# First attention of a two-block transformer kernel: far-key scores issued one round earlier, GpSimd's scaling written as a product

## The reference

```python
def block_fn(args):
    q_b, iq_b, iw_b, t_b = args
    ...
    score = jnp.where(causal[None], score, -jnp.inf)
    _, idx = lax.top_k(score, k_top)
    valid = idx <= t_b[None, :, None]
    k_sel = gather(k, idx)
    v_sel = gather(v, idx)
    logits = jnp.einsum("bthd,btkd->bhtk", q_b, k_sel).astype(jnp.float32) * (HEAD_DIM ** -0.5)
    bias = rel_bias[rel_bucket(t_b[None, :, None] - idx)]
    logits = logits + jnp.moveaxis(bias, -1, 1).astype(jnp.float32)
    logits = jnp.where(valid[:, None], logits, -jnp.inf)
    p = jax.nn.softmax(logits, axis=-1).astype(v.dtype)
    o = jnp.einsum("bhtk,btkd->bthd", p, v_sel)
```

## Time and profile before

| | |
|---|---|
| Median of 3 runs | 2642.52 us (2640.56 to 2645.78) |
| Profiled execution | 2639.89 us, span 2638.1 us |
| PE busy | 2502.7 us, 95% |
| DVE, ACT, POOL busy | 1677.6, 955.5, 655.4 us |
| Chain that ended last | PE 80%, DVE 10%, ACT 4% |

### The profile page before, as it was taken

How to read it: one execution, slowest core, us unless ns; L and a number is a source line. 1 busy time by engine, 2 the same in 40 slices (tenths; PEclk the granted TensorE clock), 3 DMA queues, 4 the chain that set the end, 5 groups by cost and what they waited for, 6 DMA issues and landing times.

```text
span 2638.1 us, 32127 instructions
## 1 busy us (share of the span) xinstructions
PE 2502.7 (95%) x12224; PEld 2062.3 (78%) x12224; DVE 1677.6 (64%) x2841; ACT 955.5 (36%) x1767; POOL 655.4 (25%) x536
## 2 busy tenths in 40 slices
PE   5999999988999899999999998999999998999998
PEld 4778888777787678888888886888877776888987
DVE  5499999477424887877654449486596566104843
ACT  4431211377323323223312243332244245225842
POOL 2147522367443000000000130000000044334753
PEclk7999999999999999999999999999999998999999
DMA  4102333200454265664533142323346123533242
GB/s 169 49 22 68 95 97 96 56 2 9 152 183 132 79 211 172 190 191 143 186 119 126 44 133 64 112 72 104 112 175 233 47 64 120 175 111 110 101 155 101
DMA packets 263172, 302.11 MB, mean 115 GB/s; under 512 B 11144, under 2 KB 216428, under 8 KB 263020
## 3 DMA queue, kind: packets, MB, share of 16 engines
q1 hardware_dynamic: 263020, 300.05, 35.0%
HBM read 228.15 MB, written 70.29 MB: 113 GB/s over the span
## 4 chain that ended last, share of the span: by engine, by line
PE 80%; DVE 10%; ACT 4%; DMA 2%; issue 2%; POOL 1%; SPq 0%; POOLq 0%; DVEq 0%; ACTq 0%
PE ps L67 78%; PE ps L70 2%; DVE tmp L79 2%; ACT tmp L73 1%; DVE sm L79 1%; DVE tmp L76 1%; ACT pth L73 1%; DVE wl L76 1%; DVE pwa L76 1%; DVE B2l L76 1%; DVE X L79 0%; DVE ptl L79 0%; ACT bh L73 0%; DVE bl L79 0%; ACT wh L73 0%
## 5 line engine op out<-in xcount | busy, mean ns | idle before, releaser
L76 POOL TENSOR_TENSOR wl<-raw,wh 128x512 fp32r<-128x512 f32 (+1 forms) x224 | 291.0, 1320 | 1590.6 <-ACT wh L73 1590.4
L73 ACT ACTIVATE wh<-raw 128x512 fp32r<-128x512 f32 (+1 forms) x388 | 226.4, 621 | 241.9 <-PE ps L67 177.1
L67 PE MATMUL ps<-B2h,wh 128*128 128x512 f32 x616 | 244.4, 397 | 13.6 <-DVE B2l L76 7.1
L67 PE MATMUL ps<-B2l,wh 128*128 128x512 f32 x616 | 241.4, 392 | 0.0
L67 PE MATMUL ps<-B2h,wl 128*128 128x512 f32 x616 | 241.3, 392 | 0.0
L73 ACT ACTIVATE tmp<-ps 128x512 f32<-128x512 f32 (+5 forms) x164 | 119.2, 738 | 332.3 <-PE ps L67 317.7
L76 DVE TENSOR_TENSOR tmp<-tmp,ps 128x512 f32<-128x512 f32 x204 | 138.4, 685 | 108.4 <-PE ps L67 92.7
L67 PE MATMUL ps<-ah,wh 128*128 128x512 f32 (+1 forms) x608 | 192.1, 393 | 14.0 <-DVE xt L85 9.9
L73 ACT ACTIVATE wh<-ws 128x512 fp32r<-128x512 f32 x152 | 94.4, 627 | 289.2 <-DVE ws L76 262.1
L67 PE MATMUL ps<-B3h,wh 128*128 128x512 f32 x448 | 178.5, 398 | 15.2 <-DVE B3l L76 7.2
L67 PE MATMUL ps<-al,wh 128*128 128x512 f32 (+1 forms) x608 | 190.7, 391 | 0.0
(11 more groups left out here) (290 smaller groups left out, 5785.8 us busy)
## 6 DMA issues: line engine op xcount, KB each, us to landing
ada<-in_ada_w SPq DMA_DIRECT2D x48, 512.0 KB, 3.8
raw<-in_w_in SPq DMA_DIRECT2D x37, 512.0 KB, 4.5
raw<-in_a_w_in SPq DMA_DIRECT2D x33, 512.0 KB, 4.4
gates<-tmp SPq DMA_DIRECT2D x32, 512.0 KB, 3.0
raw<-in_w_ffn_gate SPq DMA_DIRECT2D x24, 512.0 KB, 5.6
hd<-tmp SPq DMA_DIRECT2D x22, 512.0 KB, 4.6
gf<-hd SPq DMA_DIRECT2D x22, 512.0 KB, 7.2
raw<-in_a_w_out SPq DMA_DIRECT2D x20, 512.0 KB, 3.4
```

What stands on the lines that cost most here:

```text
L67: return self.e.matmul(*a, **k) if self.e else Ins()
L73: return self.e.activation(*a, **k) if self.e else Ins()
L76: return self.e.tensor_tensor(*a, **k) if self.e else Ins()
```

## The change

The function `score` of PE now makes one part at a call. Its near part (or the only part, for b below 2) is made at the head of round n as before. Its far part is made by a second entry of the pipeline with lag -1, which stands behind `turn` and ahead of both `values`: so in round n-1. Waits and PSUM ring are the same. On POOL, `norm` is a `tensor_tensor` product with the share spread along the row by `to_broadcast` in place of a `tensor_scalar`.

```diff
-        def score(n):
+        def score(n, part=None):
 
             b, hd = self.ITEMS1[n]
-            if n % 2:
+            parts = self.parts1(b)
+            if n % 2 or part is None and len(parts) == 1:
                 return
...
-            for part, (s0, s1) in enumerate(self.parts1(b)):
-                ps = [self.take(e, ("s", n + k, part), ring=self.p_score) for k in (0, 1)]
...
+            at = 0 if part is None else len(parts) - 1
+            s0, s1 = parts[at]
+            ps = [self.take(e, ("s", n + k, at), ring=self.p_score) for k in (0, 1)]
...
-        pipeline(64, [(0, score), (4, turn), (6, lambda n: values(n, 1)), (5, lambda n: values(n, 0))])
+        pipeline(64, [(0, lambda n: score(n, "near")), (4, turn), (-1, score), (6, lambda n: values(n, 1)), (5, lambda n: values(n, 0))])
...
-                e.tensor_scalar(L[:, 0:W], L[:, 0:W], self.st1(n)[3], None, ALU.mult).then_inc(
+                e.tensor_tensor(L[:, 0:W], L[:, 0:W], self.st1(n)[3].to_broadcast([128, W]), ALU.mult).then_inc(
```

More of the change, by code:

```diff
@@ L1563, in score @@
             c, qh, ql = slice(b * 128, b * 128 + 128), self.qh[hd // 2], self.ql[hd // 2]
-            for part, (s0, s1) in enumerate(self.parts1(b)):
-                ps = [self.take(e, ("s", n + k, part), ring=self.p_score) for k in (0, 1)]
[L1566 to L1569, removed]
+            at = 0 if part is None else len(parts) - 1
+            s0, s1 = parts[at]
+            ps = [self.take(e, ("s", n + k, at), ring=self.p_score) for k in (0, 1)]
+            for i, (q, k) in enumerate(((qh, self.KH), (qh, self.KL), (ql, self.KH))):
+                for p, r in zip(ps, (slice(0, 64), slice(64, 128))):
+                    ins = e.matmul(p[:, 0:s1 - s0], q[r, c], k[r, s0:s1], start=i == 0, stop=i == 2)
+            ins.then_inc(self.sig["prod"].up(*(("prod", ("s", n + k, at)) for k in (0, 1))), 1)
         def turn(n):
```

## The result

The changed kernel takes 2684.5 us (median of 4 executions, 2677.8 to 2688.9); the kernel before took 2641.5 in the same comparison. The ratio is 1.0161, 95% interval 1.0147 to 1.0175: 43 us slower. The forecast had the sign, but 21.9 us of it, and a range that ended at 2669.

The account below looks back on a forecast made before the run. PE, busy 95% of the span, was taken to bound the kernel. Terms 5.1 - 0.4 + 17.2 = 21.9 us on 2639.89 gave 2661.8, with the median's 2.6 us 2664.4; forecast 2663, range 2650 to 2669.

Parts of the forecast that it names:

- The far scores come to wait for `top_far`: On PE in round n-1, far(n) waits for DVE's `top_far` of item n-1: some 20 waits, 0.4 to 1 us each.
- Pairs n = 0 mod 4: First attention, far part ahead of values products on the path: eleven pairs cost 0.21 to 0.62 us, sum 5.1 us.
- Pairs n = 2 mod 4: Far part leaves ACT's shadow and delays values products ACT awaits: 1.12 to 1.70 us per pair, together 17.2 us.
- Sum 21.9 us: Whole first attention: 5.1 - 0.4 + 17.2 us of added time from moving the far parts.
- the list: The prediction's prices per pair for far parts moved a round sooner, such as 0.62 for pair 56, 1.42 for 58.
- The idle before the second part: PE's idle before item 47's second part of the turn: grows from 1.4 to about 2.1 us.
- POOL's product is covered: POOL's scaling falls to 1.9 us at 1024 columns but saves nothing, since a 2.3 us margin before PE's turn covers it.
- rival 4: PE's clock falls as its idles become 2 us: one fall of 10 us costs some 5 us, 2668; chance 0.04.
- Rivals 1 to 3: Waits vanish, lengths count: about +5 (0.06); turn releases ACT: 2642 to 2647 (0.04); faster through POOL: 2628 (0.02).

Follow-up runs that it names:

- e6: The changed kernel with unread matmuls in PE's idles ahead of early far scores and before every fourth transpose's second part: 2667.5 us, ratio 1.0098.
- e1: The kernel before with only POOL's scaling changed to the tensor_tensor product, order of the scores as before: 2641.8 us, ratio 0.9997.
- e5: The changed kernel with unread matmuls only in PE's waits just ahead of each early far score: 2675.8 us.
- e7: The kernel before with 17 unread matmuls in PE's 4.2 us idle at the start of the attention: 2641.3 us, ratio 0.9998.
- e12: The kernel before with far scores sooner only for pairs n = 2 mod 4, plus unread matmuls ahead of them and in the turns' idles: 2664.0 us, ratio 1.0078.
- e3: The kernel before with far scores sooner only for pairs n = 0 mod 4, POOL as before: 2653.3 us, ratio 1.0041.

## Why the prediction was right or wrong

- *The far scores come to wait for `top_far`, behind which stand the values products.* Right: 23 waits, 16.9 us; the longest is 1.9 us, where 1 was forecast.
- *Pairs n = 0 mod 4: 0.61 us each at full width.* Right to the hundredth in the idle (0.61 and 0.61), a little small in its effect: from the turn's second part to ACT's next copy it is 6.67 us (661.66 to 668.33) instead of 5.83, 0.84 more and not 0.62.
- *Pairs n = 2 mod 4: 1.42 for pair 58.* 1.54: from 668.33 to 673.14 are 4.81 us, from 631.21 to 634.48 were 3.27.
- *Sum 21.9 us.* With the clock held up (`e6`) it is 25.8; pair by pair the list was 14% short (21.1 against 18.5), in part because a far part holds PE for 0.9 us and not 0.80. With this error alone the time would have been that of `e6`, 2667.5, inside the range.
- *The idle before the second part grows from 1.4 to about 2.1 us.* Wrong: 1.58 and 1.68 us at 661.66 and 677.44. It did not change the sum.
- *POOL's product is covered.* Right (`e1`). Its price, 1.9 us, was right too. The rule of the Trainium skill (GPSIMD Engine Reference, "Performance versus the Vector engine") that two inputs cost more than one did not hold for this pair of forms: 1892 against 2842 ns.
- *The clock, which the sum holds at 1.00, and rival 4, "One fall of 10 us costs some 5 us: 2668. Chance 0.04".* This is the step that failed. The sum has no term for the clock, and the rival's was too small: the clock did not fall once but in nine stretches after 540 us, and stood 53.5 us longer at half speed than before, which cost 17 us. I had taken the 1.00 of the kernel before as a reason against a fall, though the new order adds idles to the old ones. At narrow widths, where PE before had waited 0.8 to 1.1 us for `ptl`, it now waits longer for the far scores' banks:

```profile
561.46 0.50 PE L67 MATMUL ps<-kp,qh 64*128 64x256 f32 x4 [1.55 <-DVE st L88]
...
572.61 1.00 PE L67 MATMUL ps<-kp,qh 64*128 64x384 f32 x4 [1.69 <-DVE st L88]
...
586.34 1.01 PE L67 MATMUL ps<-kp,qh 64*128 64x384 f32 x4 [1.93 <-DVE st L88]
```

The six matmuls of 384 columns at 586.34 run at half clock (1.01 us for the first four) and those at 580.75 took 0.62. Behind the idle of 1.55 us the clock goes down as well:

```profile
562.50:567.50 5.00, 4.61 (x29) 3.92 (x27) 1.70 (x7) 1.85 (x5) 2.08 (x3) 0.70 0.00 0
```

At wide widths the falls follow the old idle with a new one close behind it; the far scores of 512 columns then take 1.22 us instead of 0.73:

```profile
613.02 0.33 PE L70 MATMUL ps<-ident,tmp 128*128 128x128 f32 x1 [1.37 <-DVE ptl L79]
613.92 1.22 PE L67 MATMUL ps<-kp,qh 64*128 64x512 f32 x4 [0.56 <-DVE st L88]
```

But no length of an idle tells a fall from none: idles of 1.44 and 1.51 us in the kernel before (625.38, 652.63) passed without one, and so did 1.58 followed by 0.61 at 661.66, while in `e5`, with the far scores' waits filled, the clock fell behind 1.26 us (590.62). What decides is not shown.

- *Rivals 1 to 3* did not come about. ACT's copies still wait for the products (68.7 us in 24 pieces, where it was 28.0 in 24), and no filled idle gave anything back.

If PE alone were on the path, a us at half clock would cost 0.5 us. Here it cost 0.34: in the profiled executions the stage of the changed kernel ends 17.3 us behind that of `e6`, with 50.9 us more at half clock; `e7` got back 2.8 for 9. A likely reason, not tested, is that ACT and DVE stand on the path too, and their rows are as long as before.

The 5.7 us lost behind the stage are not traced to the change. All kernels run the same code there, and in the fourteen profiled executions it takes 1964.1 us (before) to 1970.9 (`e5`), in no order of what was changed: 1969.8 in the changed kernel, 1964.9 in `e6`, 1969.1 in `e12`. Whether that is chance is not shown. For `e12` this is the 5 us by which its time lies above its stage. What stays open is `e3`: its stage ends 13.4 us late, and list and clock together (4.7, and 0.34 times 14.4) make some 10.

## What to carry to other kernels

Before moving work of the bounding engine into a place behind a wait, look at who waits for what stands behind it, and price each such place from the releaser's row. Then ask a second question that a list of delays does not answer: is the engine idle longer or more often, and does the granted clock, now 1.00, still hold with that? Where it might not, give the fall of the clock over the whole stage a case of its own and a chance to match; and to find out which part of a loss it is, fill the idles with matmuls that nobody reads.

## What the runs showed of the hardware

- With no idle longer than 1.93 us, the granted clock of the changed kernel went down to 0.50 nine times between 540 and 715 us; in the kernel before, with idles of up to 1.51 us, it stayed at 1.00 from 535 us to the end of the stage. The Trainium skill (TensorE: Matmul & The Clock Gate, "HAM oscillation — how this bites in real kernels") warns of idles longer than any of these; the runs show that shorter ones can do it, as its "A second HAM failure mode: psum-queue depth-cycling" tells of another kernel.
- Matmuls whose result nobody reads, put into the idles, kept it at 1.00 from 540 us on, and made a kernel with more instructions 17 us faster.
- On GpSimd a float32 product with one number spread along the row took 1892 ns for 1024 columns and 400 ns for 128; the scaling with the number as a scalar 2842 and about 605.
